# Recurrence units of an RWKV-7 mixer: the transposed inverse made by VectorE's 32x32 transposes, and convolution taps dealt out over ten steps

## The reference, cut to what matters

```
def step(S, inp):
    r_t, w_t, k_t, v_t, a_t, b_t = inp
    sa = jnp.einsum("bhvk,bhk->bhv", S, a_t)
    S = S * w_t[:, :, None, :] + sa[..., None] * b_t[:, :, None, :] + v_t[..., None] * k_t[:, :, None, :]
    y = jnp.einsum("bhvk,bhk->bhv", S, r_t)
    return S, y
...
c = u[..., :D_CONV] * jax.nn.sigmoid(u[..., D_CONV:])
c = _causal_dwconv(c, cconv_w, cconv_b)       # 31 taps
c = jax.nn.silu(_layer_norm(c, cln_g, cln_b))
```

## Time and profile before

| | |
|---|---|
| median of three runs | 1777.9 us (1777.76 to 1782.23) |
| span of the profiled execution | 1776.4 us |
| PE busy over the span | 96% |
| DVE, ACT, POOL busy over the span | 57%, 43%, 54% |
| recurrence units (from L of the first pair to the end of U of the last) | about 175 to 335 us |

### The profile page before, as it was taken

One profiled execution on the slowest core, in us unless ns is written; L12 is line 12 of the kernel. 1 busy time (PEld: TensorE's weight loads), 2 busy tenths in 40 slices (PEclk: granted clock), 3 DMA queues, 4 the chain that ended last, 5 costly groups with the idle time before them and its releaser, 6 DMA issues.

```text
span 1776.4 us, 26816 instructions
## 1 busy us (share of the span) xinstructions
PE 1697.5 (96%) x10602; PEld 1393.1 (78%) x10602; DVE 1014.9 (57%) x1276; ACT 763.0 (43%) x1261; POOL 954.4 (54%) x758
## 2 busy tenths in 40 slices
PE   8999999989799999999998999999989999999987
PEld 7677999867488888888787777776877888888765
DVE  4697544575655555201455666667485666666575
ACT  4553767422333333101433565567134444444572
POOL 4443777767099999999356022224554444444062
PEclk9999999989899999999999999999999999999998
DMA  5221000233022222424112000001331111111211
GB/s 191 72 95 48 2 1 2 97 145 157 33 75 101 102 100 94 166 101 170 50 48 72 25 24 1 25 0 57 110 155 48 48 47 44 45 45 46 88 68 48
DMA packets 18870, 126.38 MB, mean 71 GB/s; under 512 B 2096, under 2 KB 2352, under 8 KB 4304
## 3 DMA queue, kind: packets, MB, share of 16 engines
q1 hardware_dynamic: 18624, 124.41, 19.1%
q10 hardware_dynamic: 144, 0.52, 0.1%
HBM read 122.83 MB, written 2.10 MB: 70 GB/s over the span
## 4 chain that ended last, share of the span: by engine, by line
PE 51%; issue 19%; POOL 16%; DVE 9%; ACT 3%; DMA 0%; POOLq 0%; ACTq 0%; DVEq 0%; SPq 0%
POOL w_hi L648 8%; PE banks L1233 5%; POOL cacc L670 4%; PE banks L1212 4%; POOL w_lo L639 3%; PE banks L1390 3%; PE banks L1393 3%; PE banks L1391 3%; PE banks L1095 3%; PE banks L1100 3%; PE banks L1096 3%; PE banks L751 2%; PE banks L1445 2%; PE banks L752 2%; PE banks L753 2%
## 5 line engine op out<-in xcount | busy, mean ns | idle before, releaser
L648 POOL TENSOR_TENSOR w_hi<-raw,der 128x512 fp32r<-128x512 f32 x296 | 341.0, 1162 | 455.8 <-PE banks L1393 184.9
L639 POOL TENSOR_TENSOR w_lo<-raw,w_hi 128x512 fp32r<-128x512 f32 x336 | 468.9, 1408 | 65.9 <-ACT w_hi L1536 65.9
L751 PE MATMUL banks<-h_hi,w_hi 128*128 128x512 f32 x496 | 198.7, 401 | 5.6 <-DVE h_lo L2368 5.3
L752 PE MATMUL banks<-h_lo,w_hi 128*128 128x512 f32 x496 | 194.4, 392 | 0.0
L753 PE MATMUL banks<-h_hi,w_lo 128*128 128x512 f32 x496 | 194.2, 392 | 0.0
L1390 PE MATMUL banks<-h_hi,w_hi 128*128 128x512 f32 (+1 forms) x384 | 146.8, 382 | 0.1
L1391 PE MATMUL banks<-h_lo,w_hi 128*128 128x512 f32 (+1 forms) x384 | 131.5, 358 | 0.0
L2019 ACT ACTIVATE dP<-banks,der 128x768 f32<-128x768 f32 x64 | 57.7, 902 | 159.9 <-DVE der L2772 159.9
L751 PEld LDWEIGHTS banks<-h_hi,w_hi 128*128 128x128 f32 x496 | 93.6, 189 | 35.1 <-issue 12.7
L1393 PE MATMUL banks<-h_hi,w_lo 128*128 128x512 f32 (+1 forms) x384 | 116.5, 358 | 0.0
L698 POOL TENSOR_TENSOR Of<-Of,Ls 128x768 f32<-128x768 f32 x8 | 14.7, 1833 | 186.7 <-DVE Ls L2574 186.7
(11 more groups left out here) (491 smaller groups left out, 4152.5 us busy)
## 6 DMA issues: line engine op xcount, KB each, us to landing
raw<-in_stream SPq DMA_DIRECT2D x84, 1024.0 KB, 4.8
ada_raw<-in_ada_w SPq DMA_DIRECT2D x18, 1024.0 KB, 6.9
raw<-in_ada_w SPq DMA_DIRECT2D x4, 1024.0 KB, 4.8
xT<-in_x_t SPq DMA_DIRECT2D x2, 1024.0 KB, 6.1
xT<-in_x_t SPq DMA_DIRECT2D x1, 2048.0 KB, 7.9
ada_end<-in_ada_w SPq DMA_DIRECT2D x2, 1024.0 KB, 5.8
out_t<-z SPq DMA_DIRECT2D x8, 256.0 KB, 2.1
ctxT<-in_ctx_t SPq DMA_DIRECT2D x1, 1024.0 KB, 6.8
```

Source lines behind the costliest of these rows:

```text
L639: return pool.tensor_tensor(lo[:, h, part(i), :], raw_tiles(half)[:, part(i), :], hi[:, h, part(i), :], ALU.subtract)
L648: pool.tensor_tensor(hi[:, h, part(i), :], raw_tiles(half)[:, part(i), :], one, ALU.mult).then_inc(hi_done, 1)
L751: pe.matmul(banks[b][:, :], hi, tile(rhs_hi, k), start=(at_k == 0), stop=False)
L752: pe.matmul(banks[b][:, :], hi, tile(rhs_lo, k), start=False, stop=False)
```

## The change

Two things change, both in the same stage.

First, the transpose. Q1 to Q4 leave PE, and the placing of their results leaves DVE. In their place DVE takes a STREAM_TRANSPOSE of `Di` into `DiT` behind each P (steps T1 to T4), which transposes every 32x32 block in its place. At the start L and ACT's DI are dropped too: DVE places LT's blocks in `DiT` (DT0) and then transposes `DiT` into `Di` (D0). P of level n waits for T of level n - 1, Q5 for T4. PE's first step is now LT, and it waits for U's copy of the pair before, where L waited for W's.

Second, the taps. They still are 24 a pair, but two or three stand behind each of ten steps of ACT: LT, MV, Y0, G1 to G5, W and U.

```diff
-    PE_STEPS = ["L", "LT", "MT", "RB", "RK", "MV", "Y0"] + [s + str(n) for n in range(1, 6) for s in "GPQ"][:-2] + ["Q5", "W", "U"]
-    ACT_STEPS = ["DI", "DIT", "LT", "MV", "Y0", "G1", "G2", "G3", "G4", "G5", "W", "U"]
-    DVE_STEPS = ["D0", "DT0", "MT", "RB", "RK"] + [s + str(n) for n in range(1, 5) for s in "PQ"] + ["Q5"]
+    PE_STEPS = ["LT", "MT", "RB", "RK", "MV", "Y0"] + [s + str(n) for n in range(1, 5) for s in "GP"] + ["G5", "Q5", "W", "U"]
+    ACT_STEPS = ["DIT", "LT", "MV", "Y0", "G1", "G2", "G3", "G4", "G5", "W", "U"]
+    DVE_STEPS = ["DT0", "D0", "MT", "RB", "RK"] + [s + str(n) for n in range(1, 5) for s in "PT"] + ["Q5"]
...
-            if step == "L":
+            if step == "LT":
...
-                    pe.wait_ge(u_act[e], act_at(c - 1, "W"))
-                b, lhs, rhs = X[0], eA[rows, c, :], aB[rows, c, :]
-            elif step == "LT":
-                if c:
                     pe.wait_ge(u_act[e], act_at(c - 1, "U"))
                 b, lhs, rhs = X[1], aB[rows, c, :], eA[rows, c, :]
...
-                    pe.wait_ge(u_dve[e], dve_at(c, f"Q{n - 1}" if n > 1 else "DT0"))
+                    pe.wait_ge(u_dve[e], dve_at(c, f"T{n - 1}" if n > 1 else "DT0"))
                     b, lhs, rhs = X[1], DiT[e], Gt[e]
                 else:
-                    if n == 1:
-                        pe.wait_ge(u_dve[e], dve_at(c, "RK"))
                     pe.wait_ge(u_act[e], act_at(c, f"G{n}"))
-                    if n == 5:
-                        pe.wait_ge(u_dve[e], dve_at(c, "Q4"))
+                    pe.wait_ge(u_dve[e], dve_at(c, f"T{n - 1}"))
...
+        TAPS_BEHIND = {"LT": 3, "MV": 2, "Y0": 2, "G1": 3, "G2": 2, "G3": 3, "G4": 2, "G5": 3, "W": 2, "U": 2}
...
-                if step == "LT" or step[0] == "G":
-                    for i in range(next_tap, next_tap + 4):
-                        tap(i)
-                    next_tap += 4
+                n_taps = TAPS_BEHIND.get(step, 0)
+                for i in range(next_tap, next_tap + n_taps):
+                    tap(i)
+                next_tap += n_taps
...
+            def turned(out, src):
+
+                dve.transpose(out[:, :, :].rearrange("p a b -> p (a b)"), src[:, :, :].rearrange("p a b -> p (a b)")).then_inc(u_dve[e], 1)
...
-            elif step == "D0":
-                dve.wait_ge(u_pe[e], pe_at(c, "L"))
-                dve.wait_ge(u_act[e], act_at(c, "DI"))
-                placed(Di[e], bank(0), 0)
             elif step == "DT0":
                 dve.wait_ge(u_act[e], act_at(c, "LT"))
                 placed(DiT[e], bank(1), 6)
+            elif step == "D0":
+                dve.wait_ge(u_dve[e], dve_at(c, "DT0"))
+                turned(Di[e], DiT[e])
+            elif step[0] == "T":
+                dve.wait_ge(u_dve[e], dve_at(c, "P" + step[1]))
+                turned(DiT[e], Di[e])
```

More of the change, by code:

```diff
@@ L1644, in unit @@
             rows, h = slice(64 * e, 64 * e + 64), 2 * c + e
-            if step in ("DI", "DIT"):
+            if step == "DIT":
                 if c:
@@ L1649, in unit @@
                     act.wait_ge(block_done, N_IN)
-                act.activation((Di if step == "DI" else DiT)[e][:, :, :], ident4, ACT.Copy).then_inc(u_act[e], 1)
+                act.activation(DiT[e][:, :, :], ident4, ACT.Copy).then_inc(u_act[e], 1)
                 return
```

## The result

Over 20 runs of each, the changed kernel takes 1785.33 us and the kernel before 1779.26 us; the ratio is 1.0029, 95% interval 1.0016 to 1.0042. The prediction was 1771.4 us, in a range that ended at 1781: it came out slightly slower instead of faster. The profiled execution of the changed kernel has a span of 1785.9 us, 9.5 over the one before; that difference is what is taken apart here. It is larger than the 6.1 us between the medians, since each is a single execution: one of the slower ones of the changed kernel (1787.7) and one under the median of the kernel before.

A forecast was written before the change was run, and what follows sets the result against it. TensorE's own work was taken to set the recurrence stage's pace. A net -12.6 us at full clock plus 6.1 us of clock loss gave -6.5 us, from 1777.9 to 1771.4 us; range 1764 to 1781.

The forecast's parts named there:

- Level: One level of the inverse, G to next G, without Q: 3.83 us instead of 5.42, saving 6.36 us a pair.
- Transpose: VectorE's transpose over 512 columns: 0.70 us, hidden behind TensorE's products and not stretched by GpSimd's additions.
- (b): Rival: transpose dearer by width, near 1.1 us, levels just exposed; result about 1776 to 1778 us; chance 0.08.
- (c): Rival: GpSimd's additions stretch each transpose to 1.65 us, VectorE bounds the level; slower, 1790 to 1795 us; chance 0.09.
- RK: Head of a pair: RK starts at +6.2 us, 1.17 later than before, with TensorE idle some 2.4 us ahead of it.
- G1's copy held: Taps on ScalarE's queue hold the copy of G1, so P1 comes 1.0 us late in each pair.
- U's hand-over: Between pairs, LT now waits for U's copy, which taps behind W and U may hold: +0.35 us a pair.
- Stage at full clock: Recurrence stage without clock loss: TensorE leaves it some 16.4 us earlier, from -3.84 us a pair and the first pair's head.
- End of the stage: GpSimd's last additions end later: chain starts 5.7 us after U instead of 1.90, giving back 3.8 us.
- Clock: TensorE's clock halves behind gaps in three of four heads (4.35 us) and at chain start (1.7): +6.1 us, ends 0 and 8.
- 3.4 us of it lose 1.45 us: Length of one fall in a head: 3.4 us at half clock, weight products 1.74 times as long, costing 1.45 us.
- Rival (d): The clock falls in all heads and stays down longer: gain only 3 to 5 us, 1773 to 1775 us; chance 0.18.

The follow-up runs named there:

- the run with filled heads: Changed kernel plus 16 unread products a pair on TensorE between RB and RK, in the gap before RK; 1774.37 us, 0.9969 of the kernel before.
- work behind RK: Changed kernel plus the same 16 unread products a pair, placed behind RK so the gap before it stays; 1789.3 us, 1.0054 of the kernel before.
- masks first: Changed kernel with VectorE's masks on M, RB and RK ahead of placing DiT and its transpose; 1760.99 us, 0.9906 of the kernel before.

## Why the prediction was wrong

Step by step, against the profile of the changed kernel and, for full clock, the run with filled heads.

- **Level:** forecast 3.83, measured 3.83. Right.
- **Transpose:** forecast 0.70, hidden, not stretched; measured 0.69, longest 0.71, and no P product waits for one. The transposes' rows in the section on the result also bear on the rule that was weighed against the state update's row: the Trainium skill (SBUF — State Buffer, Who interferes with whom) has a one-input operation free of contention with GpSimd, and 40 transposes from 661 to 706 ns beside 115 us of additions agree. Rivals (b) and (c) are out.
- **RK:** forecast +6.2 with 2.4 us idle; measured +6.16 and 2.42. Right.
- **G1's copy held:** forecast +1.0; P1 follows G1 by 3.21 us at full clock instead of 1.85, +1.36. The sum gave Y0's two copies 0.97 us and the two taps behind them 1.23; with filled heads they occupy ScalarE for 1.22 and 1.36.
- **U's hand-over:** forecast +0.35; LT waits 0.52 for the copy of U, and the pairs that have this wait are 0.58 longer than the last one (36.40, 35.82). Undersized by 0.2.
- **Stage at full clock:** forecast -16.4; measured 145.14 - 159.67 = -14.5. With the end of the stage, the net gain without the clock was 10.6 us, not 12.6.
- **End of the stage:** forecast 5.7 us between U and the chain, measured 5.79: +3.9.
- **Clock:** forecast +6.1, with 8 as the upper end; measured 155.79 - 145.14 = 10.65 us in the stage and 8.5 in the chain, together 19.1. **This is the step that failed.** That the clock would fall, in heads and at the chain's start, was right. What failed is "3.4 us of it lose 1.45 us": a fall lasted 10.2 us in a head and 23.9 at the chain's start. Each of the three heads lost 3.4 to 3.9 us, and the chain 8.5 instead of 1.7. That three of four heads would fall was a choice between what two rows allowed, and that it came out is partly luck: an earlier fall, which the forecast didn't have, had shrunk the first head's gap to 0.80 us, and that is probably why it was spared. In four experiments the first head has a gap before RK of 1.25 to 2.36 us, and the clock falls behind it.

The sum of the measured terms is -14.5 + 3.9 + 10.65 + 8.5, which with +1.6 and -0.6 from outside the stage gives the 9.5 us between the two profiles. With the forecast's other terms and the measured clock the answer would have been some 6 us slower, on the right side. Rival (d), the clock falling in all heads and for longer, named the mechanism, but its -3 to -5 us leave the clock only 7.6 to 9.6 us, and the forecast's end was 8.

The size could have been seen beforehand. The length of a fall was taken from one stretch of 3.3 us, and the longer falls of rival (d) were given no length. In the kernel before, the chain stage has one twice as long, behind an idle stretch of only 1.45 us:

```profile
362.50:369.20 6.70, 6.70 (x98) 5.86 (x97) 4.02 (x11) 0.00 (x0) 6.70 (x7) 0.50 0.51 175
```

An upper end made of a whole head, RK to G1, at half clock would have been 4 us for each head (5.24 us times 0.74) and as much again for a slow chain step, an estimate of some 20 us in all, and the range would have reached to about 1785.

The Trainium skill has a case of this kind (TensorE: Matmul & The Clock Gate, A second HAM failure mode: psum-queue depth-cycling): in one kernel of bf16 products of 512 columns, frequent very short idles between groups of matmuls made the clock swing between its two levels, at a cost in throughput. The rows above agree that short gaps are enough, down to 1.13 us, in fp32 products of 64x128.

What stays open: why a fall lasted 3.4 us in some heads and 10.2 in others, and why one gap of 1.1 us brings it and the next doesn't. With work behind RK all three falls lasted 3.4 us, which speaks for a part played by what runs after the gap; but within one kernel, too, falls behind like gaps last 7.0 and 10.4 us, and no run here measures by what law.

## What to carry to other kernels

A shortened dependency chain on the engine that sets the pace can leave small idle stretches in other places, and each may cost more than its own length through the clock (here 2.23 us of idle time before RK cost 3.4 to 3.9 us more, 4.69 before the chain 8.5); look for every place where TensorE will newly wait a microsecond or more, take as the upper case a stretch at half clock as long as those seen here (10 us in a head, 24 at the start of the chain), and compare that sum with the gain. Then close the gaps by order rather than by work: here moving three masks ahead of a placing that nobody waited for, and four taps out of the last pair's end, turned a loss of 0.3% into a gain of 1.7%. Where it is unclear whether latency or the clock eats a gain, fill the gap with products that nobody reads: if the kernel gets faster, it was the clock.

## What the runs showed of the hardware that was not expected

- Adding 64 products to the program, 16 in the gap of each pair, made it 11 us faster (1785.3 to 1774.4); the same 64 behind the gap made it 4 us slower (1789.3).
- Before the chain, an idle stretch of 2.9 us was followed by 23.4 to 23.8 us at 1.2 GHz (two runs), one of 4.7 us by 13.5 to 13.8 us in three runs and by 23.7 to 23.9 in three others, the changed kernel among them: the length of the gap doesn't set the length of the fall.
- Gaps of 1.13 to 1.25 us among products of 64x128 went with a fall in three of four heads, gaps of 1.17 us among products of 128x128 in none of the pairs with masks first. A gap of 1.55 us among products of 64x128 went with a fall in two pairs and with none in a third.
- A 128x512 fp32 transpose by 32x32 blocks from SBUF to SBUF takes 0.69 us on VectorE, as much as a mask out of PSUM (0.68), and ran so beside GpSimd's additions (661 to 706 ns).
